# Three of the five shared-expert down products made inside the expert loop, kept in SBUF, and added by VectorE at the end

## The chip, the cores and the metric

One core of a Trainium2 chip runs the whole program. The time is the device time of one execution in microseconds (us); lower is better. TensorE is called PE here, VectorE DVE, ScalarE ACT, GpSimd POOL, and SyncE, whose queue issues most of the large DMAs, SP.

## What is computed

One layer of a decoder trunk over 512 prompt tokens and 8 sample tokens, 1024 wide: a token mixer with two gated convolution branches, then a mixture of experts with 64 routed experts (8 for each token) and one shared expert. All in float32. The part that the change touches is the end of the second half:

```
hg = jnp.einsum('td,edf->tef', h, p['w1'])
hu = jnp.einsum('td,edf->tef', h, p['w3'])
act = jax.nn.silu(hg) * hu * gate[:, :, None].astype(h.dtype)
routed = jnp.einsum('tef,efd->td', act, p['w2'])
shared = (jax.nn.silu(h @ p['ws1']) * (h @ p['ws3'])) @ p['ws2']
return routed + shared
...
x = x + gt2 * rmsnorm(f, p['g_post2'])
```

## The kernel before

The program has a first half (projections, convolutions, router), an expert loop and a tail. Each engine has its own program; they meet at semaphores.

**The expert loop.** The rows of each expert are cut into strips of 64, and one pass handles two strips that follow each other (128 rows). For these inputs there are 49 passes. In a pass, POOL gathers the rows from `h2_rows` into `xg`; PE transposes them (`rows_T`, L1684) into PSUM banks 0 and 1; PE makes the up products with w1 and w3 (`up_product`, L1691) into banks 2 and 3, transposes the gated result (`act_T`, L1697) into banks 6 and 7, and makes the down products with w2 (`down_products`, L1703) into banks 4 and 5. ACT evicts those, and POOL scatters them to `y_rows` in HBM. PE's code for this loop is `for u in range(DEEP): expert(g * DEEP + u, u, g)` in a hardware loop over `g` of 10 turns: six bodies written out one behind the other, one for each slot of weights, and four more bodies for the last four experts. A body is skipped where its expert has no pass to make, and repeated where it has several. Which experts have how many passes follows from the routing of the inputs.

**The weights.** SP loads 3 MB for each expert (`up_weights`, two DMAs of 1 MB at L351; `down_weights`, one at L356) into six slots. `refill` waits until the expert six back has finished (semaphores `ex3` and `ex_y` against a pass number) before it overwrites that slot.

**The shared expert.** Its up products and gating are done before the loop; the result waits in `scr`. Its down products (`shared_down`, L1770, 4 matrix products of 128 x 128 by 128 x 512 for each token tile) are made in the tail, where PE opens the PSUM sum of each tile with them. `ws2` (1 MB) is loaded at L410, late in the loop, into a slot that is free by then.

**The tail.** There are five token tiles: four of 128 prompt tokens and one of 8 sample tokens. Tile n has two PSUM banks, `bank_of = (6, 0, 2, 4, 6)`. PE adds to the shared product the gated rows that were scattered to `y_rows`: eight rows a token, in a first and a last half (`gated_rows`, L1778, with h=1 from `y_first` and h=0 from `y_last`), each half a load of 2 MB by `tile_rows` (L406) into places in the weight slots. For each finished tile ACT squares and sums (L987) and takes the root (L990), DVE takes the reciprocal (L1363), scales (L1369) and adds the residual (L1372), and SP stores it (L452). SP's loads wait for the last pass that wrote rows of the tile (`rows_there`), for the slot (`slot_free`), and where a place is used twice, for PE's `early_pe`.

Of the kernel before, what the change touches and what calls it, by code (L numbers as in the profile page):

```python
# [10 lines left out]
ALU = mybir.AluOpType  # L11
ACT = mybir.ActivationFunctionType
AX = mybir.AxisListType
ds = bass.ds
# [8 lines left out]
def build_program(  # L23
# [33 lines left out]
    with ctx:  # L57
# [64 lines left out]
        hx = ring[:, 0, 4 * D:6 * D].rearrange("p (b d) -> p b d", b=2)  # L122
        hflat = act5[:, R:2 * R]
        yb = hflat[:, 2 * D:4 * D].rearrange("p (b d) -> p b d", b=2)
        gmat = hflat[:, 0:D].rearrange("p (b i h m) -> p b i h m", b=4, i=TT - 1, h=2)
        xflat = act5[:, 0:R]
# [12 lines left out]
        sel, selm, repl = (xflat[:, o + n * RE:o + (n + 1) * RE].rearrange("p (i e) -> p i e", i=TT) for n in range(3))  # L139
# [21 lines left out]
        outb = [hflat[:, D:2 * D], slot_part(4, YF, D), slot_part(4, YF + D, D)]  # L161
# [60 lines left out]
        def s8(n):  # L222
# [45 lines left out]
                 "m_hi_dve x1_pool gp_pe gm_dve early_dve early_pe last_pass_dve x1t_T x1t_done x1t_dve h2_dve oneE_dve token_act turn_pool sh_mm sh_ev sh_act "  # L268
# [34 lines left out]
        def _(sp):  # L303
# [71 lines left out]

            def refill(e, before, u):
# [33 lines left out]
            sp.dma_start(ws2_back, w_src(ws2, 0, D)).then_inc(w_late, 16)  # L410
            slot_free(E - 5)
            x1_back(0)
            x1_back(1)
# [10 lines left out]
            for i in range(3):  # L424
                tile_rows(y_first, i, 1, y_first_in)
# [3 lines left out]
            tile_rows(y_first, 3, 1, y_first_in)  # L429
# [3 lines left out]
            sp.dma_start(G2, g2_rows[0:1, :].to_broadcast([P, D])).then_inc(g2_in, 16)  # L433
            rows_there(1)
            tile_rows(y_last, 0, 0, y_last_in[0])
            slot_free(E - 2)
            sp.dma_start(G2s, g2_rows[1:NSEQ, :]).then_inc(g2_in, 16)
            rows_there(2)
            tile_rows(y_last, 1, 0, y_last_in[1])
            rows_there(3)  # L440
            slot_free(E - 1)
            tile_rows(y_last, 2, 0, y_last_in[2])
            rows_there(4)
            sp.wait_ge(S["early_pe"], 1)
            tile_rows(y_last, 3, 0, y_last_in[3])
# [216 lines left out]
        def _(act):  # L662
# [321 lines left out]
            for n in range(TT):  # L984
                rows, f = (P if order[n] < TT - 1 else LAST), bank_of[n]
                act.wait_ge(S["stat_mm"], 3 * C + n + 3)
                act.activation(sflat[0:rows, 0:D], ps[0:rows, f:f + 2, :].rearrange("p b n -> p (b n)"), ACT.Square,  # L987
# [5 lines left out]
        def _(dve):  # L993
# [287 lines left out]
            link(dve.tensor_reduce(red[0:1 + TT, 2:3], ps[0:1 + TT, 6, 0:P], AX.X, ALU.max), "early_dve", wait=False)  # L1281
            tile_no = dve.alloc_register("tile_no")
            dve.reg_mov(tile_no, 0)

# [37 lines left out]
            link(ts(last_pass, ps[0:1, 6, P:P + 1 + TT], 4.0 * P - 1.0, None, ALU.add), "early_dve")  # L1322
# [14 lines left out]
            with dve.Fori(0, pairs) as it:  # L1337
                for u in range(2):
# [18 lines left out]

            for n in range(TT):
                i, f = order[n], bank_of[n]
                rows = P if i < TT - 1 else LAST  # L1360
                buf, r = outb[n % 3][0:rows, :], nrm[0:rows, 1, n:n + 1]
# [7 lines left out]
                stt(out=buf, in0=ps[0:rows, f:f + 2, :].rearrange("p b n -> p (b n)"), scalar=r, in1=(G2 if i < TT - 1 else G2s)[0:rows, :],  # L1369
# [5 lines left out]
        def _(pe):  # L1375
# [344 lines left out]
            for n in range(3):  # L1720
                pe.reg_load(next_steps[n], steps_of[0:1, n:n + 1])
# [121 lines left out]
```

## Time and profile before

| | us |
|---|---|
| median of 3 runs | 1288.71 |
| lowest and highest | 1286.37 and 1288.80 |
| the profiled execution, device time | 1286.83 |
| its span in the profile | 1285.1 |
| expert loop, first to last matrix product of PE | 644.1 to 1242.4 |
| tail, to the end | 1242.4 to 1285.1 |

"Idle before" in a row is time in which that engine had nothing to run just before those instructions, with what ended it. "Issue" is time in which the engine waited for nothing that the profile shows. PEld is PE's weight load, which overlaps PE; PEldq and PEq are its sequencer. A busy PE in the profile counts pipelined matrix products, so it can read 100% of a stretch. The DMA share is the mean busy share of 16 DMA engines. An instruction packet (queue q8) brings 16 KB of PE's code, 256 instructions of 64 bytes. The program's instructions by the written order are 7517 for PE, 29.4 packets, and 29 packets are seen.

### The profile page before, as it was taken

How to read it: one execution, taken by the hardware profiler on the slowest of the kernel's cores; microseconds unless marked ns; L12 is line 12 of the kernel's file. 1: busy time of each engine (PE TensorE's matmuls, PEld its weight loads, DVE VectorE, ACT ScalarE, POOL GpSimd, SP SyncE). 2: the span in 40 equal slices, each digit the busy share in tenths (PEclk: the TensorE clock that was granted, in tenths of full speed). 3: DMA queues.
4: the chain of work that ended last, by engine and by line, in shares of the span. 5: the costliest groups of instructions: out<-in, count | busy, mean ns of one | idle time of the engine just before them, and what ended most of it. 6: DMA issues, size and time to landing. Idle time of an engine off the chain costs nothing.

```text
span 1285.1 us, 26379 instructions
## 1 busy us (share of the span) xinstructions
PE 1222.1 (95%) x9371; PEld 912.3 (71%) x9372; DVE 466.3 (36%) x840; ACT 344.5 (27%) x628; POOL 375.6 (29%) x380
## 2 busy tenths in 40 slices
PE   5699999999999999977999999999799999999997
PEld 4599999999999999966755655555455565555552
DVE  0566686658566538226722111101000100110114
ACT  4332322322333531335211212112112121211212
POOL 1144544445447234320412122122112212212210
PEclk9799999999999999987989999999899999999999
DMA  9944253452421133408699999999999999999883
GB/s 305 291 159 153 83 194 103 147 159 82 147 82 49 34 104 93 132 1 322 260 360 382 369 365 420 391 418 418 418 417 418 391 406 361 416 419 410 340 339 141
DMA packets 157770, 337.33 MB, mean 262 GB/s; under 512 B 12390, under 2 KB 96870, under 8 KB 141328
## 3 DMA queue, kind: packets, MB, share of 16 engines
q1 hardware_dynamic: 140048, 295.55, 61.2%
q0 software_dynamic: 14256, 34.10, 7.0%
q10 hardware_dynamic: 3424, 7.09, 1.7%
q8 instruction: 29, 0.48, 0.2%
q14 instruction: 13, 0.11, 0.0%
HBM read 322.21 MB, written 33.30 MB: 277 GB/s over the span
## 4 chain that ended last, share of the span: by engine, by line
PE 82%; DMA 5%; issue 5%; DVE 4%; POOL 2%; SPq 1%; ACT 1%; DVEq 0%; ACTq 0%; POOLq 0%
PE ps L1691 26%; PE ps L1703 13%; PE ps L1456 10%; PE ps L1457 9%; PE ps L1458 9%; PE ps L1684 4%; DMA w<-in_w_dram 2%; DMA ring<-in_w_ada_dram 2%; PE ps L1770 1%; PE ps L1469 1%; PE ps L1697 1%; PE ps L1411 1%; PE ps L1778 1%; PE ps L1636 1%; PE ps L1399 1%
## 5 line engine op out<-in xcount | busy, mean ns | idle before, releaser
L1691 PE MATMUL ps<-w,xe 128*64 x3136 | 351.4, 383 | 12.8 <-DMA w<-in_w_dram 8.9
L1691 PEld LDWEIGHTS ps<-w,xe 128*64 128x64 f32 x3136 | 228.1, 138 | 148.5 <-issue 44.7
L520 POOL TENSOR_TENSOR wsplit<-ring,wsplit 128x1024 fp32r<-128x1024 f32 x80 | 192.2, 2402 | 302.4 <-ACT wsplit L713 302.4
L1456 PE MATMUL ps<-h_s_hi,wsplit 128*128 128x260 f32 x960 | 272.2, 284 | 0.0
L1458 PE MATMUL ps<-h_s_hi,wsplit 128*128 128x260 f32 x960 | 270.7, 282 | 0.0
L1457 PE MATMUL ps<-h_lo_m_hi,wsplit 128*128 128x260 f32 x832 | 234.8, 282 | 0.0
L1334 DVE TENSOR_TENSOR rs<-sg,ps 128x128 f32<-128x128 f32 x98 | 23.8, 284 | 480.8 <-PE ps L1691 480.8
L1456 PEld LDWEIGHTS ps<-h_s_hi,wsplit 128*128 128x128 f32 x960 | 180.6, 188 | 6.7 <-issue 6.7
L1458 PEld LDWEIGHTS ps<-h_s_hi,wsplit 128*128 128x128 f32 x960 | 180.8, 188 | 0.0
L1703 PE MATMUL ps<-w,eactT 128*64 (+1 forms) x784 | 179.0, 598 | 0.0
L713 ACT ACTIVATE wsplit<-ring 128x1024 fp32r<-128x1024 f32 x80 | 84.8, 1060 | 310.1 <-PE ps L1458 294.2
L1457 PEld LDWEIGHTS ps<-h_lo_m_hi,wsplit 128*128 128x128 f32 x832 | 156.6, 188 | 0.0
L1072 DVE SCALAR_TENSOR_TENSOR ps<-conv,vecs,ps 128x512 f32<-128x512 f32 x224 | 154.7, 745 | 0.0
L595 POOL COPY gidx<-idxT 128x1 int32 (+1 forms) x50 | 9.4, 189 | 395.7 <-PE ps L1684 394.3
L1703 PEld LDWEIGHTS ps<-w,eactT 128*64 128x64 f32 x784 | 52.2, 136 | 89.7 <-issue 83.7
L955 ACT ACTIVATE act<-ps 128x1024 f32<-128x1024 f32 x50 | 51.2, 1023 | 162.9 <-PE ps L1703 147.3
L970 ACT ACTIVATE eactT<-ps 128x128 f32<-128x128 f32 x98 | 23.3, 277 | 188.6 <-PE ps L1697 188.6
L1684 PE MATMUL ps<-ident,scr 128*128 128x128 f32 x400 | 65.7, 287 | 0.0
L1684 PEld LDWEIGHTS ps<-ident,scr 128*128 128x128 f32 x400 | 52.3, 193 | 18.9 <-issue 17.7
L598 POOL DMA_INDIRECT scr<-h_rows,gidx x50 | 53.1, 1063 | 39.7 <-POOL gidx L595 39.7
L608 POOL DMA_INDIRECT y_rows<-act,sidx x49 | 50.4, 1028 | 40.3 <-POOL sidx L605 32.1
L967 ACT ACTIVATE sg<-ps 128x256 f32<-128x256 f32 x49 | 18.8, 384 | 134.5 <-PE ps L1691 132.0
(315 smaller groups left out, 1363.3 us busy)
## 6 DMA issues: line engine op xcount, KB each, us to landing
w<-in_w_dram SPq DMA_DIRECT2D x192, 1024.0 KB, 15.3
ring<-in_w_in_dram SPq DMA_DIRECT2D x56, 512.0 KB, 3.7
ring<-in_w_ada_dram SPq DMA_DIRECT2D x12, 2048.0 KB, 8.9
act<-y_rows SPq DMA_DIRECT2D x4, 2048.0 KB, 10.2
ring<-y_rows SPq DMA_DIRECT2D x4, 2048.0 KB, 9.5
ring<-in_w_out_a_dram SPq DMA_DIRECT2D x8, 512.0 KB, 3.5
ring<-in_w_out_b_dram SPq DMA_DIRECT2D x8, 512.0 KB, 3.6
ring<-in_w_o_dram SPq DMA_DIRECT2D x8, 512.0 KB, 3.5
```

What stands on the lines that cost most here:

```text
L520: pool.tensor_tensor(wsplit[:, b, 1], raw[raw_slot], wsplit[:, b, 0], ALU.subtract).then_inc(S["w_lo"], 1)
L598: pool.indirect_dma_start(out=xg, out_offset=None, in_=h2_rows, in_offset=bass.IndirectOffsetOnAxis(ap=gidx[:, u:u + 1], axis=0), bounds_c ...
L608: pool.indirect_dma_start(out=y_rows, out_offset=bass.IndirectOffsetOnAxis(ap=sidx[:, u:u + 1], axis=0), in_=yb[:, u, :], in_offset=None, ...
L713: act.activation(wsplit[:, b, 0], raw[raw_slot], ACT.Copy).then_inc(S["w_hi"], 1)
L955: act.activation(yb[:, 1 - u, :], ps[:, 4:6, :].rearrange("p b n -> p (b n)"), ACT.Copy).then_inc(S["ex_yd"], 1)
L1072: chain(stt(out=acc[k % 2] if k != KC - 2 else cvj, in0=glu[:, k:k + NP], scalar=vecs[:, ds(j + (V_WC + 8 * k), 1)], in1=acc[k % 2], op0=A ...
L1456: mm(ps[:, bank + h, 0:HT], wsplit[:, b, 0, k, :], hi[:, k, p:q], start=(k == 0), stop=False)
L1457: mm(ps[:, bank + h, 0:HT], wsplit[:, b, 0, k, :], lo[:, k, p:q], start=False, stop=False)
L1458: ins = mm(ps[:, bank + h, 0:HT], wsplit[:, b, 1, k, :], hi[:, k, p:q], start=False, stop=(k == C - 1))
L1684: ins = tr(ps[:, h, (c % 4) * P:(c % 4 + 1) * P], v[:, c, :], ident[:, :])
L1691: ins = mm(ps[a * STRIP:(a + 1) * STRIP, bank, 0:FE], xe[:, k, a * STRIP:(a + 1) * STRIP], w[a][:, k, :], start=(k == 0), stop=(k == C - 1))
L1703: ins = mm(ps[a * STRIP:(a + 1) * STRIP, 4 + h, :], eactT[:, k, a * STRIP:(a + 1) * STRIP], w[a][:, k, h * 512:(h + 1) * 512], start=(k == ...
```

## The change

`ws2` is loaded before the loop, into two new places, instead of late in it. In passes 11, 12 and 13 (p = 10, 11, 12) PE makes the down products of token tiles 1, 2 and 3 behind the down products of the pass, into PSUM banks 6 and 7, and DVE copies them to SBUF (`xflat`). Each of the ten bodies of PE's code holds the three products behind comparisons with the pass number. In the tail `gated_rows` opens the PSUM sum of tiles 1 to 3, and DVE adds the parked product to it; the sum stands in SBUF, and ACT and DVE read it from there. Tiles 0 and 4 are made as before. The places of `y_first` and `y_last` move: the second half of tile 1 is now in slot 4, and the second halves of tiles 2 and 3 in slots 5 and 0, each behind one step of `early_pe`. Names of semaphores change with that (`early_dve` is now `sums_dve`).

```diff
-        y_first = [blocks(t) for t in (xflat[:, 0:YF], slot_part(5, 0, YF), slot_part(0, 0, YF), slot_part(1, 0, YF))]
-        y_last = [blocks(t) for t in (slot_part(2, 0, YF), slot_part(3, 0, YF), slot_part(4, 0, YF), xflat[:, 0:YF])]
-        ws2_back = slot_part(5, YF, 2 * D).rearrange("p (k n) -> p k n", k=FT)
+        y_first = [blocks(slot_part(n, 0, YF)) for n in (5, 0, 1, 2)]
+        y_last = [blocks(slot_part(n, 0, YF)) for n in (3, 4, 5, 0)]
+        FIRST_SH = 10
+        SH_TILES = TT - 2
...
             sp.wait_ge(S["table_dve"], 1)
 
+            for k in range(FT):
+                sp.dma_start(ws2_late[k], ws2[0, k * P:(k + 1) * P, :]).then_inc(w_late, 16)
+
...
-            sp.dma_start(ws2_back, w_src(ws2, 0, D)).then_inc(w_late, 16)
...
-            rows_there(4)
-            sp.wait_ge(S["early_pe"], 1)
-            tile_rows(y_last, 3, 0, y_last_in[3])
+            for i in range(2, TT - 1):
+                rows_there(i + 1)
+                sp.wait_ge(S["early_pe"], i - 1)
+                tile_rows(y_last, i, 0, y_last_in[i])
...
                     one_pass(p)
+                    with dve.If(it > FIRST_SH // 2 - 1):
+                        with dve.If(it < FIRST_SH // 2 + 2 - u):
+                            n = dve.snap(shared_no, min_val=1, max_val=SH_TILES)
+                            dve.wait_ge(S["late_chain"], LA * TT)
+                            dve.wait_ge(S["sh_mm"], n + 2 * FT)
+                            dve.tensor_copy(xflat[:, ds(n * D - D, D)], ps[:, 6:8, :].rearrange("p b n -> p (b n)")).then_inc(S["sums_dve"], 1)
+                            dve.wait_ge(S["sums_dve"], n + 2)
+                            dve.reg_add(shared_no, shared_no, 1)
...
+            def with_shared(n):
+
+                if n > SH_TILES:
+                    return
+                f, total = bank_of[n], xflat[:, (n - 1) * D:n * D]
+                dve.wait_ge(S["stat_mm"], 3 * C + n + 3)
+                tt(total, total, ps[:, f:f + 2, :].rearrange("p b n -> p (b n)"), ALU.add).then_inc(S["sums_dve"], 1)
+
             for n in range(TT):
                 i, f = order[n], bank_of[n]
                 rows = P if i < TT - 1 else LAST
+                if n > 0:
+                    with_shared(n + 1)
...
+            def shared_in_loop(i):
+
+                pe.wait_ge(w_late, 16 * C + 64)
+                for h in range(2):
+                    for k in range(FT):
+                        ins = mm(ps[:, 6 + h, :], scr[:, 2 + k, i * P:(i + 1) * P], ws2_late[k][:, h * 512:(h + 1) * 512],
+                                 start=(k == 0), stop=(k == FT - 1))
+                ins.then_inc(S["sh_mm"], 1)
...
                         down_products(down, 1).then_inc(S["ex_y"], 1)
+                        with pe.If(p > FIRST_SH - 1):
+                            with pe.If(p < FIRST_SH + SH_TILES):
+                                with pe.If(p < FIRST_SH + 1):
+                                    shared_in_loop(1)
+                                with pe.If(p > FIRST_SH):
+                                    with pe.If(p < FIRST_SH + 2):
+                                        shared_in_loop(2)
+                                    with pe.If(p > FIRST_SH + 1):
+                                        shared_in_loop(3)
...
             pe.wait_ge(S["xe_dve"], passes + 1)
-            shared_down(1)
+            mark(gated_rows(1, 1, y_first), "early_pe")
             last_sums(0)
-            gated_rows(1, 1, y_first)
             pe.wait_ge(S["ex_yd"], passes + 2)
             for n in range(2, TT - 1):
-                shared_down(n)
+                gated_rows(n, 1, y_first)
                 last_sums(n - 1)
-                gated_rows(n, 1, y_first)
```

On PE, at the end of each body of the expert loop, before (L1703 are the down products, L1730 and L1729 the ends of the pass loop and of the body):

```order
L1703 ISA [waits ea_act]
L1703 MATMUL ps<-w,eactT 64x512 x2
L1703 ISA
L1703 MATMUL ps<-w,eactT 64x512 x2
L1730 REGISTER_ALU
L1730 COMPARE_AND_BRANCH
L1729 UNCONDITIONAL_BRANCH
```

The same place now (L1736 are the down products, L1761 the shared ones):

```order
L1736 MATMUL ps<-w,eactT 64x512 x2
L1797 COMPARE_AND_BRANCH
L1798 COMPARE_AND_BRANCH
L1799 COMPARE_AND_BRANCH
L1761 MATMUL ps<-act,scr 128x512 [waits w_late]
L1761 MATMUL ps<-act,scr 128x512 x3
L1799 UNCONDITIONAL_BRANCH
L1801 COMPARE_AND_BRANCH
L1802 COMPARE_AND_BRANCH
L1761 MATMUL ps<-act,scr 128x512 [waits w_late]
L1761 MATMUL ps<-act,scr 128x512 x3
L1802 UNCONDITIONAL_BRANCH
```

Behind these rows stands a third copy (L1804), and then the loop ends as before. A product of this kind is four instructions on the engine (two weight loads and two matrix products), so a body grows by 48 of them and 9 branches, from 221 to 278 instructions.

On PE in the tail, before, from the shared product of tile 0 on:

```order
L1770 MATMUL ps<-act,scr 128x512 [waits w_late]
L1770 MATMUL ps<-act,scr 128x512 x3
L1778 MATMUL ps<-act 32x512 [waits y_first_in,gm_dve]
L1778 MATMUL ps<-act 32x512 x7
L1800 REGISTER_ALU
L1770 MATMUL ps<-act,scr 128x512 [waits xe_dve,xe_act]
L1770 MATMUL ps<-act,scr 128x512 x3
L1778 MATMUL ps<-ring,act 32x512 [waits y_last_in0]
L1778 MATMUL ps<-ring,act 32x512 x7
L1778 MATMUL ps<-act 32x512 x8
L1805 REGISTER_ALU
L1770 MATMUL ps<-act,scr 128x512 [waits ex_yd]
```

And now:

```order
L1821 MATMUL ps<-act,scr 128x512 [waits w_late]
L1821 MATMUL ps<-act,scr 128x512 x3
L1829 MATMUL ps<-act 32x512 [waits y_first_in,gm_dve]
L1829 MATMUL ps<-act 32x512 x7
L1851 REGISTER_ALU
L1829 MATMUL ps<-ring,act 32x512 [waits xe_dve,xe_act]
L1829 MATMUL ps<-ring,act 32x512 x7
L1829 MATMUL ps<-ring,act 32x512 [waits y_last_in0]
L1829 MATMUL ps<-ring,act 32x512 x7
L1855 REGISTER_ALU
L1829 MATMUL ps<-ring,act 32x512 [waits ex_yd]
```

The shared products of tiles 1 to 3 are gone from between the gated rows; that of tile 4 stays.

## Rows read from the trace of the kernel before

**Rows 1.** The page: span, busy time of PE, and PE's code packets.

```profile
span 1285.1 us, 26379 instructions
PE 1222.1 (95%) x9371; PEld 912.3 (71%) x9372; DVE 466.3 (36%) x840; ACT 344.5 (27%) x628; POOL 375.6 (29%) x380
...
q8 instruction: 29, 0.48, 0.2%
```

**Rows 2.** Chain that ended last, passes 47 and 48: start us, us, what.

```profile
1218.55 6.91 PE ps L1691 x64
...
1230.48 6.91 PE ps L1691 x64
```

**Rows 3.** Chain that ended last, tail.

```profile
1243.59 3.63 PE ps L1770 x8
...
1252.71 3.57 PE ps L1778 x32
...
1275.90 1.12 ACT scr L987 x2
```

**Rows 4.** Groups by line, 1242 to 1286: busy us, mean ns, idle before.

```profile
L1369 DVE SCALAR_TENSOR_TENSOR act<-ps,nrm,ring 128x1024 f32<-128x1024 f32 (+1 forms) x5 | 6.4, 1281 | 0.2
L1372 DVE TENSOR_TENSOR act<-act,ring 128x1024 f32<-128x1024 f32 (+1 forms) x5 | 6.1, 1223 | 0.2
```

**Rows 5.** Chain around the wait for weights.

```profile
873.36 6.91 PE ps L1691 x64
...
888.86 28.71 DMA w<-in_w_dram
918.27 9.11 PE ps L1691 x64
...
932.41 6.91 PE ps L1691 x64
```

**Rows 6.** Loads of weights issued at 713 and at 827: median us to landing.

```profile
w<-in_w_dram SPq DMA_DIRECT2D x2, 1024.0 KB, 8.7
...
w<-in_w_dram SPq DMA_DIRECT2D x3, 1024.0 KB, 12.3
```

**Rows 7.** Stretches: busy us of each engine, PE's clock, DMA share, GB/s.

```profile
749.00:755.00 6.00, 6.00 (x38) 3.16 (x38) 1.74 (x7) 1.77 (x4) 2.44 (x4) 1.00 0.80 319
791.00:803.00 12.00, 12.00 (x94) 6.95 (x92) 1.18 (x3) 2.37 (x5) 2.44 (x4) 1.00 1.02 419
```

**Rows 8.** Loads in 1242 to 1275: median us from issue to landing.

```profile
act<-y_rows SPq DMA_DIRECT2D x2, 2048.0 KB, 10.2
```

**Rows 9.** PE's code packets: 0 to 136, 640 to 700, 646.5 to 648.

```profile
q8 instruction: 7, 0.11, 0.4%
...
q8 instruction: 5, 0.08, 0.6%
...
q8 instruction: 1, 0.02, 4.9%
```

**Rows 10.** Queues of 136 to 411 us, then of 700 to 1188: all there are.

```profile
q1 hardware_dynamic: 48878, 32.51, 37.9%
...
q1 hardware_dynamic: 30173, 169.37, 85.3%
q0 software_dynamic: 11554, 27.20, 14.4%
```

**Rows 11.** Branches that skip a body, at 643 and at 1192: ns min/median/max, start us.

```profile
L1729 PEldq COMPARE_BRANCH  x2: 70/204/337, 643.0 to 643.6; - x2
L1729 PEldq COMPARE_BRANCH  x2: 65/196/328, 1192.0 to 1192.5; - x2
```

**Rows 12.** DMA of 1193 to 1195 us: PE's code packet.

```profile
q8 instruction: 1, 0.02, 3.3%
```

**Rows 13.** Line 1691 in pass 48: matrix products, and the sequencer's work for them.

```profile
L1691 PE MATMUL ps<-w,xe x64: 379/379/379, 1230.3 to 1237.0; 128*64 x32, 128*64 128x256 f32 x32
L1691 PEldq FUSED_REGOPS  x16: 42/46/51, 1228.0 to 1234.6; - x16
```

More of the change, by code:

```diff
@@ L138, in build_program @@
         o += 4 * TT * 8
-        sel, selm, repl = (xflat[:, o + n * RE:o + (n + 1) * RE].rearrange("p (i e) -> p i e", i=TT) for n in range(3))
+        repl, sel, selm = (xflat[:, o + n * RE:o + (n + 1) * RE].rearrange("p (i e) -> p i e", i=TT) for n in range(3))
         rank1, place_of = sel, repl
@@ L267, in build_program @@
                  "g_done m_done m_chain t_cp stat_mm sqd idx_ab idx_mm hx_T hx_done "
-                 "m_hi_dve x1_pool gp_pe gm_dve early_dve early_pe last_pass_dve x1t_T x1t_done x1t_dve h2_dve oneE_dve token_act turn_pool sh_mm sh_ev sh_act "
+                 "m_hi_dve x1_pool gp_pe gm_dve sums_dve early_pe last_pass_dve x1t_T x1t_done x1t_dve h2_dve oneE_dve token_act turn_pool sh_mm sh_ev sh_act "
                  "exT xe_act xe_dve ex1 ex3 ex_sil ex_mul exA ea_act "
@@ L423, in _ @@
             rows_there(0)
-            for i in range(3):
-                tile_rows(y_first, i, 1, y_first_in)
+            tile_rows(y_first, 0, 1, y_first_in)
+            slot_free(E - 5)
+            x1_back(0)
+            x1_back(1)
+            tile_rows(y_first, 1, 1, y_first_in)
             slot_free(E - 4)
@@ L985, in _ @@
                 rows, f = (P if order[n] < TT - 1 else LAST), bank_of[n]
-                act.wait_ge(S["stat_mm"], 3 * C + n + 3)
-                act.activation(sflat[0:rows, 0:D], ps[0:rows, f:f + 2, :].rearrange("p b n -> p (b n)"), ACT.Square,
+                if 1 <= n <= SH_TILES:
+                    act.wait_ge(S["sums_dve"], 2 + SH_TILES + n)
+                    total = xflat[:, (n - 1) * D:n * D]
+                else:
+                    act.wait_ge(S["stat_mm"], 3 * C + n + 3)
+                    total = ps[0:rows, f:f + 2, :].rearrange("p b n -> p (b n)")
+                act.activation(sflat[0:rows, 0:D], total, ACT.Square,
                                accum_out=nrm[0:rows, 0, n:n + 1]).then_inc(S["fin_sq"], 1)
@@ L1280, in _ @@
             link(tt(first_at, beyond, one64[0:1, :], ALU.add), "table_dve")
-            link(dve.tensor_reduce(red[0:1 + TT, 2:3], ps[0:1 + TT, 6, 0:P], AX.X, ALU.max), "early_dve", wait=False)
+            link(dve.tensor_reduce(red[0:1 + TT, 2:3], ps[0:1 + TT, 6, 0:P], AX.X, ALU.max), "sums_dve", wait=False)
             tile_no = dve.alloc_register("tile_no")
             dve.reg_mov(tile_no, 0)
+            shared_no = dve.alloc_register("shared_no")
+            dve.reg_mov(shared_no, 1)
             def token_tile(i, u):
@@ L1368, in _ @@
                     dve.wait_ge(tile_out[n % 3], 16)
-                stt(out=buf, in0=ps[0:rows, f:f + 2, :].rearrange("p b n -> p (b n)"), scalar=r, in1=(G2 if i < TT - 1 else G2s)[0:rows, :],
+                total = xflat[:, (n - 1) * D:n * D] if 1 <= n <= SH_TILES else ps[0:rows, f:f + 2, :].rearrange("p b n -> p (b n)")
+                stt(out=buf, in0=total, scalar=r, in1=(G2 if i < TT - 1 else G2s)[0:rows, :],
                     op0=ALU.mult, op1=ALU.mult).then_inc(S["yacc"], 1)
@@ L1372, in _ @@
                 tt(buf, buf, x1b[i][0:rows, :], ALU.add).then_inc(S["fin_out"], 1)
+                if n == 0:
+                    with_shared(1)
         @block.tensor
@@ L1769, in shared_down @@
                     for k in range(FT):
-                        mm(ps[0:rows, f + h, :], scr[:, 2 + k, i * P:i * P + rows], ws2_back[:, k, h * 512:(h + 1) * 512],
+                        mm(ps[0:rows, f + h, :], scr[:, 2 + k, i * P:i * P + rows], ws2_late[k][:, h * 512:(h + 1) * 512],
                            start=(k == 0), stop=False)
@@ L1778, in gated_rows @@
                         ins = mm(ps[32 * b:32 * b + 32, f + c, :], gmat[:, b, i, h, :], src[i][:, b, c * 512:(c + 1) * 512],
-                                 start=False, stop=(h == 0))
+                                 start=(h == 1 and 1 <= n <= SH_TILES), stop=(h == 0))
                 return ins
@@ L1794, in _ @@
             mark(ins, "gp_pe")
-            pe.wait_ge(w_late, 16 * C + 48)
+            pe.wait_ge(w_late, 16 * C + 64)
             shared_down(0)
```

26 lines of the change are left out of this document (12 added, 14 removed).

## Prediction

> **What bounds the kernel now.** I read the page first. PE is busy 95% of the span, DVE 36% and POOL 29% [rows 1], so the question is what PE gains, loses or waits for. Then the chain that ended last. In the expert loop it runs through PE's products, one pass starting 11.93 us after the one before (1230.48 − 1218.55) [rows 2]; 49 passes at 11.92 make 584 us of the 598.3 us from 644.1 to 1242.4. Of the other 14 us some 11.4 stand at one place: four passes from 873.36 to 932.41 take 59.05 us and not 47.7, because PE waits for a load of weights that took 28.71 us, and the products behind it take 9.11 us instead of 6.91 at a lower clock [rows 5]. In the tail the chain is PE again, shared and gated products one behind the other, until ACT squares the last tile at 1275.90, 33.5 us after the loop's end [rows 3]. Behind it ACT and DVE need 9.2 us to the end.
>
> So work taken out of the tail's PE chain shows there. Work put into passes 11 to 13 shows in full, unless the wait for weights at 890 swallows it.
>
> **The work put into the loop.** A shared product is 8 matrix products, 3.63 us in the tail [rows 3]. Three are 10.9 us. PE has no gap in those passes: the chain of the later passes has none [rows 2], and in 791 to 803 PE is busy 12.00 of 12.00 us [rows 7]. So passes 11 to 13 grow from 11.9 to 15.5 us.
>
> Does the wait for weights absorb that? The bounds are 10.9 (nothing) and −0.5 (it hands over all of its 11.4). In favour of absorbing: 85 us later PE waits for a transfer anyway. Against: SP issues a load only when PE has finished the expert six back, so PE's delay delays the issues, and the DMA engines absorb it only as far as transfers are queued. That backlog is read from the time from issue to landing: 8.7 us for loads issued at 713, 12.3 at 827 [rows 6]. So some 3.6 us are queued by then; the rest of the 10.9 us the DMA engines stand idle, and what they don't move in time is missing at 890. I take 10.9 − 3.6 = **+7.3 us**.
>
> Three smaller edits I cost at nothing, with their cover. The comparisons: one to nine branches for each pass, 65 to 70 ns where not taken and 328 to 337 ns where taken [rows 11]; PE's sequencer ends its work for L1691 at 1234.6, when the products end at 1237.0 [rows 13], a lead of 2.2 to 2.4 us, and uncovered they would be about 0.3 us a pass (49 × 0.3 = 15 us, which I don't expect). DVE's copy of 128 x 1024 from PSUM is like L1372 (1.22 us [rows 4]); DVE is idle most of a pass, and banks 6 and 7 are wanted again by PE's `act_T` over 7 us later; the wait for `sh_mm` has only the next pass's gating queued behind it, and that needs products which PE makes later. The early load of `ws2`: 1 MB, some 2.5 us of all engines at 419 GB/s; the DMA share is 0.80 in 749 to 755 [rows 7], so room is there before anything waits, and its late load is gone.
>
> **The tail.** PE loses three products, 3 × 3.63 = 10.9 us: the last sum is ready 22.6 us after the loop's end instead of 33.5. DVE gets three additions of 128 x 1024 (1.22 to 1.28 us each [rows 4]), the one for tile n+1 in front of the scaling of tile n. With PE sending a tile every 3.57 us [rows 3] and DVE needing 0.17 + 1.28 + 1.22 + 1.25 = 3.9 us for each, DVE becomes the engine that sets the pace from tile 1 to 3. Laid out by hand: the additions and the slower pace cost 2.8 us of the 10.9, so the tail gains **8.1 us**. The loads of gated rows are next in line. One took 10.2 us [rows 8]; the second half of tile 1 now waits for the last pass and lands about 8 us behind the loop's end (wanted at 12), that of tile 2 at 14 (wanted at 15.7), tile 3 at about 20 (wanted at 21). They just hold. Bounds: 10.9 if the additions vanish in gaps, 5 if the loads come 3 us late.
>
> **The sum without anything else** is +7.3 − 8.1 = −0.8 us: nothing.
>
> **PE's code.** The change also makes the loop's code longer, and that I take to decide. The code comes in packets of 256 instructions [rows 9]. Counted in the written order, the first half's loop lies from 1.6 to 7.3 packets behind the start: 7 packets, and one more that is called ahead. 7 came in 0 to 136 us [rows 9] and one at its exit; in 136 to 411 none came [rows 10]. The six bodies of the expert loop lie from 19.3 to 24.5: 6 packets and one called ahead. Five came in 640 to 700 [rows 9], and none in 700 to 1188, while ten turns run [rows 10]. So eight packets are the most that a row shows held. With 278 instructions for a body instead of 221 the loop lies from 19.3 to 25.8. The real borders lie earlier than the count: packets start to come when PE is at about 160 of 256, with its lead at about 196, so at least 60 instructions (0.24 packets) separate the count from the real border, and the loop ends at 26.06 or later. That touches 8 packets and calls a ninth.
>
> If a ninth pushes out the oldest, that is the packet with the loop's start, and each of the 9 jumps back waits for it. When it has come, it pushes out the next, and so on, but those are called ahead while 1.3 passes of work are left. So the waits are at the jumps: 9 back, and those over the sixth body where that expert has no pass (6 of 10 turns by the routing), since they land in a packet not yet called. The price from the trace: the jump at 643.0 [rows 11], with no packet until 646.5 and then one that took 4.9% of 16 engines times 1.5 us = 1.18 us [rows 9], 4.7 us in all; the jump at 1192.0 [rows 11], with none until 1193 and one of 3.3% of 16 × 2 = 1.07 us [rows 12], 2.4 us in all. Mean 3.5 us. At a jump back the sequencer's lead of 2.2 us [rows 13] covers a part: 9 × 1.3 = 12 us. At a jump over a body the lead has been used on other branches, and I take all 3.5: 6 × 3.5 = 21 us. Together **+33 us**. Bounds: 0 if nothing is pushed out, 10 if only jumps back pay, and 60 where each fetch stands behind the loads of a saturated DMA (share 1.02 in 791 to 803 [rows 7]).
>
> The Trainium skill, "Runtime: NRT & Kernel Launch", Instruction fetch mechanics, says that PE's instruction memory has 128 KiB, 2048 instructions, filled first in, first out in blocks of 16 KiB, and that a taken branch to a page not held forces a fetch before execution goes on. That is eight packets, and the loop without refetches of nine would contradict it. The same section also says that only two lines are held; by that every turn of before would refetch too, and [rows 10] show no packet in ten turns, so here the trace decides against it.
>
> **Rivals.** *Nothing is refetched* (more than eight are held, or the real end of the loop stays in the packet before): the sum is −0.8 us, 1286 to 1288. For it: the overshoot is small, 0.06 packets by my count, and no row shows a refusal of nine. *Nothing refetched, and the wait for weights swallows the added work*: −0.5 − 8.1 = −8.6, so 1278 to 1280, faster. For it is the 11.4 us stretch [rows 5]; against it the small backlog [rows 6]. *Every packet of each turn comes late*, because fetches stand behind a full DMA: 10 turns × 6 to 8 us, over 1345. The code decides over the sign: the forecast ends on the slower side from the point where jumps cost more than 0.2 us each.
>
> **How the numbers follow.** The profiled execution took 1286.83 us, 1.9 below the median of the runs; I sum against it. Forecast: 1286.83 + 7.3 − 8.1 + 33 = **1319 us**. Chances: refetches at jumps 0.50 (about 1295 to 1335 with its bounds), nothing refetched 0.28, nothing refetched and the wait swallows 0.12, all late 0.10. The range of 1284 to 1345 leaves out the last case and most of the third. A measurement of this kernel can tell 0.2% (2.6 us) from no change; by that: faster 0.15 (the third case and a little of the second), same 0.20, slower 0.65. If only the signs hold, the forecast's own range is 1295 to 1335.
>
> **What would show it.** Code packets of PE on the page: about 31 if nothing is refetched, 60 to 100 if it is, and some between 700 and 1188. The first pass of a turn starting more than 11.93 us after the one before, by 1 to 4 us, and PE idle there with nothing that the profile shows ("issue"). Passes 11 to 13 at 15.5 us. The wait for weights, 11.4 us long now, shorter by about 3.6. The tail from the loop's end to the end 34.6 us instead of 42.7, DVE's additions at about 1.25 us, and PE not waiting for gated rows. I am wrong if the packets stay at 31: then the time is that of the rivals, and their order is settled by the start of the last pass.

## The result, and the profile after

The changed kernel takes 1292.62 us (median of 7 runs, 1291.28 to 1293.2), the kernel before 1288.31 us (7 runs): a ratio of 1.0036, 95% interval 1.0026 to 1.0046, 4.3 us slower. The profiled executions took 1292.62 and 1286.83 us; the latter is one of the faster ones of its kernel, so the two traces lie 5.8 us apart. The sign is the forecast one, the size is about a seventh of the 32 us that were forecast, and the cause is another one.

The page of the changed kernel, as [rows 1]:

```profile
span 1290.9 us, 26586 instructions
PE 1224.0 (95%) x9371; PEld 913.0 (71%) x9372; DVE 473.2 (37%) x846; ACT 344.4 (27%) x628; POOL 376.3 (29%) x380
...
q8 instruction: 31, 0.51, 0.2%
```

31 code packets for 31.4 in the written order: no packet came twice. The queues of 700 to 1188 us, as [rows 10]; there is no q8 among them:

```profile
q1 hardware_dynamic: 29562, 166.21, 84.2%
q0 software_dynamic: 11317, 26.63, 14.2%
```

So the 33 us that the prediction put on refetched code are not there. Where the 5.8 us are is read from the starts of the passes (first product of L1691, now L1724, in each pass of both traces):

| | before | after | moved by |
|---|---|---|---|
| first pass starts | 644.14 | 644.44 | +0.30 |
| pass 11 starts (two steps, at passes 5 and 9) | 765.90 | 766.63 | +0.73 |
| pass 14 starts (11.3 us lost in three passes) | 801.67 | 813.71 | +12.04 |
| pass 21 starts | 885.11 | 897.22 | +12.11 |
| pass 25 starts (behind the wait for weights) | 944.16 | 954.34 | +10.18 |
| pass 45 starts | 1182.62 | 1192.84 | +10.22 |
| pass 46 starts | 1194.54 | 1207.28 | +12.74 |
| loop ends | 1242.4 | 1255.2 | +12.8 |
| tail, from there to the end | 42.7 | 35.7 | −7.0 |

Four lines of it are the case: the products cost 11.3 us, the wait for weights gives 1.9 back, 2.5 are lost at the loop's exit, and the tail gains 7.0. The 0.7 us of the first passes are no part of it: in the profiles of the kernels below, those with added copies of code aside, pass 11 starts 0.3 to 3.7 us behind before, in no relation to the edits.

The chain in passes 11 and 12 of the changed kernel (start us, us, what), beside [rows 2]:

```profile
775.13 3.58 PE ps L1736 x16
778.72 3.63 PE ps L1761 x8
782.35 7.06 PE ps L1724 x64
...
794.42 3.63 PE ps L1761 x8
```

A product is 3.63 us, as forecast, and the up products behind it take 7.06 us instead of 6.91: 3.77 a pass. DVE's copy (3 of 1225 ns) and the branches are hidden.

The wait for weights, as [rows 5]:

```profile
901.99 25.45 DMA w<-in_w_dram
927.43 0.66 issue
928.10 9.47 PE ps L1724 x64
```

It is still there, and the low clock behind it too (9.47 us for the up products; the granted clock is 0.72 in 922 to 934). PE waited 6.5 us for weights in the loop, against 8.9 before.

At the loop's exit PE's sequencer shows the loss. The branches that skip a body in the code behind the loop (now L1771), at 1202.6 and 1206.7 us, as [rows 11]:

```profile
L1771 PEldq COMPARE_BRANCH  x2: 82/1964/3846, 1202.6 to 1206.7; - x2
```

One branch took 3.85 us where the same one took 0.33 before. A code packet arrives meanwhile (one starts at 1203.8 in the trace and takes 1.27 us); PE's next product starts at 1207.28 after 2.35 us of "issue".

The tail's chain ends otherwise than before:

```profile
1257.39 7.33 DMA y_rows<-act,sidx
...
1265.30 12.04 DMA ring<-y_rows
...
1277.38 1.97 PE ps L1829 x16
...
1279.38 1.22 DVE act L1384
...
1287.31 1.21 DVE act L1403
```

In [rows 3] it ran through PE's products; now it is the last scatter, then the last load of gated rows, then DVE's addition. PE waits 1.83 us for that load.

### The profile page after: what moved, and what is told of

Its sections match the earlier page's. It is cut to its first block, busy times and chain, and to the rows that moved or that the text cites. A ratio compares the mean times of both kernels' runs of the same rounds, so it can differ in the third digit from the quotient of the medians.

```text
span 1290.9 us, 26586 instructions
## 1 busy us (share of the span) xinstructions
PE 1224.0 (95%) x9371; PEld 913.0 (71%) x9372; DVE 473.2 (37%) x846; ACT 344.4 (27%) x628; POOL 376.3 (29%) x380
## 4 chain that ended last, share of the span: by engine, by line
PE 79%; DMA 8%; issue 5%; DVE 4%; POOL 2%; SPq 1%; ACT 1%; DVEq 0%; POOLq 0%; ACTq 0%
PE ps L1724 25%; PE ps L1736 13%; PE ps L1489 9%; PE ps L1490 9%; PE ps L1491 9%; PE ps L1717 4%; DMA w<-in_w_dram 2%; DMA ring<-in_w_ada_dram 2%; DMA scr<-h_rows,gidx 1%; PE ps L1502 1%; PE ps L1730 1%; PE ps L1444 1%; PE ps L1669 1%; PE ps L1432 1%; SPq L313 1%
## 5 line engine op out<-in xcount | busy, mean ns | idle before, releaser
L1724 PE MATMUL ps<-w,xe 128*64 x3136 | 352.0, 383 | 12.9 <-DMA w<-in_w_dram 6.5
L1724 PEld LDWEIGHTS ps<-w,xe 128*64 128x64 f32 x3136 | 227.9, 138 | 149.5 <-issue 46.1
L1736 PE MATMUL ps<-w,eactT 128*64 (+1 forms) x784 | 179.0, 598 | 0.0
L1736 PEld LDWEIGHTS ps<-w,eactT 128*64 128x64 f32 x784 | 52.2, 136 | 89.9 <-issue 84.1
```

The lines of the kernel that those rows point to most:

```text
L1724: ins = mm(ps[a * STRIP:(a + 1) * STRIP, bank, 0:FE], xe[:, k, a * STRIP:(a + 1) * STRIP], w[a][:, k, :], start=(k == 0), stop=(k == C - 1))
L1736: ins = mm(ps[a * STRIP:(a + 1) * STRIP, 4 + h, :], eactT[:, k, a * STRIP:(a + 1) * STRIP], w[a][:, k, h * 512:(h + 1) * 512], start=(k == ...
```

## Experiments

Each ratio is against runs of the kernel before made beside that kernel's own. "Changed kernel" is the kernel of the diff.

### Do the products alone make the loss?

The passes at which PE's products are made are set out of reach, so the kernel leaves the shared part of tiles 1 to 3 out of its output:

```diff
-                        with pe.If(p > FIRST_SH - 1):
+                        with pe.If(p > NEVER - 1):
...
-  dve.wait_ge(S["sh_mm"], n + 2 * FT)
-  dve.tensor_copy(xflat[:, ds(n * D - D, D)], ps[:, 6:8, :]...)
+  dve.wait_ge(w_late, 16 * C + 64)
+  dve.tensor_copy(xflat[:, ds(n * D - D, D)], ws2_late[0])
```

> The code of the three products stays in all bodies, but the comparisons never hold: no shared product of tiles 1 to 3 is made, so this part of the output is left out; DVE parks other data with a copy as long as before, and the tail is the changed one. Theory (the time of the changed kernel is products in the loop, less a little swallowed by the wait for weights, plus one late code packet at the loop's exit, less the tail): the loop's passes 11 to 13 are back at 11.92 us, the last pass starts about 11.3 - 1.9 = 9.4 us earlier than in the changed kernel, near 1233.7; the 2.4 us gap before pass 46 is still there, since the code is as long; time about 1292.6 - 9.4 = 1283. Rival (branches and early ws2 cost much of it): last pass at 1236 or later, time 1285 or more.

Measured: 1279.45 us, ratio 0.9933 (0.9916 to 0.9949). No pass reaches the number 100, and it is past the bound that the program states for the pass number: the comparisons and the products' code were dropped when the kernel was built, so the code is short again, which the page shows:

```profile
q8 instruction: 29, 0.48, 0.2%
```

The last pass starts at 1232.0, 11.1 us earlier than in the changed kernel; that is 1.7 us behind before, and it was 1.9 us behind at its first pass already. The gap before pass 46, which the expectation kept, is gone with the code. So early `ws2` and the moved loads cost nothing that can be seen in the loop. DVE's copies were not as long as before, against the expectation: from SBUF they take 683 ns each, and from PSUM in the changed kernel 1225. The whole kernel is 1288.11 − 1279.45 = 8.7 us faster than before by the medians; in the two profiles its tail is 7.4 us shorter (35.3 against 42.7). The products and their code cost 13.2 us against it. The run mixes these two causes; the next runs part them.

### The gap at the loop's exit

```diff
-            def expert(e, u, turn):
+            def expert(e, u, turn, with_products=True):
...
+                        if with_products:
                             with pe.If(p > FIRST_SH - 1):
...
-                expert(E // DEEP * DEEP + u, u, E // DEEP)
+                expert(E // DEEP * DEEP + u, u, E // DEEP, False)
```

> The changed kernel without the products' code in the four bodies behind the loop, where no pass 11 to 13 falls. Theory (PE waits at the loop's exit because a skipped body is now longer than a packet of 256 instructions, 278, and lands in a packet that was not called): the skip takes 0.33 us again instead of 3.85, pass 46 starts 11.9 us after pass 45 instead of 14.4, the time falls by 2.4 us to about 1290.2. Rival (the gap comes from where the loop's end lies against the packets, or from a full DMA queue, not from the length of the skipped body): the gap stays between 1 and 3 us.

Measured: 1290.08 us, ratio 1.0018 (1.0009 to 1.0028), 2.5 us below the changed kernel. Pass 46 starts 11.92 us after pass 45, and the same branches read:

```profile
L1771 PEldq COMPARE_BRANCH  x2: 65/196/328, 1202.1 to 1202.7; - x2
```

The six bodies of the loop are unchanged and the loop ends at the same place of the code, so the longer bodies behind the loop make the gap: the skip over one of them finds its packet not there yet, and with the short bodies it doesn't. That a length above 256 instructions alone decides is not shown. In the first turn of the changed kernel the skip over the sixth body, as long as the others, did not wait:

```profile
L1771 PEldq COMPARE_BRANCH  x1: 338/338/338, 692.6 to 692.6; - x1
```

The edit changes the length of the body and the place at which the skip lands together, and no run parts the two.

### Where the products stand before the wait for weights

`FIRST_SH` alone is changed: 10 in the changed kernel; 14, 18 and 20 here. "Still to come" is what the products do to the passes behind the start of pass 21.

```diff
-        FIRST_SH = 10
+        FIRST_SH = 18
```

> The products are made in passes 19 to 21 (p = 18 to 20), just ahead of the wait for weights. Theory (a delay of PE is swallowed only when loads are queued behind each other, since each load is issued when PE has finished a pass; at p = 10 little was queued, at p = 18 the loads take over 17 us from issue to landing): the wait swallows most of the 11.3 us, up to the 9.3 us that it lasts and 2.2 us of low clock; the last pass starts about 8 us earlier than in the changed kernel, the time is 1283 to 1286. Rival (the DMA engines bound this stretch whatever PE does, and later loads come later by as much, or PE's delay comes back as a second wait): the same loop as the changed kernel within 2 us, time 1291 to 1293.

> The products are made in passes 21 to 23 (p = 20 to 22): the first two fill the very gaps in which PE waits for weights (3.3 us and 6.0 us), the third comes behind them. Theory as in the run before it: no refill that feeds the two waits is delayed, so 3.3 + 3.8 us are swallowed at once, and of the third product and of what stays of the second gap some 4 us are paid; the last pass starts 5 to 8 us earlier than in the changed kernel, time 1284 to 1288. Rival (a later wait takes the place of the removed one): time 1291 to 1293, with a wait for weights after pass 24.

> The products are made in passes 15 to 17 (p = 14 to 16). Theory (what the wait for weights swallows is what is queued when the products are made; loads take 11.9 us from issue to landing at 820 and 16 to 17 at 860, against 8 when nothing is queued): between the two cases measured, 3 to 6 us swallowed, last pass near 1239 to 1241, time 1287 to 1290. Rival (swallowed is all or nothing, by whether the products stand inside some 40 us ahead of the wait): as passes 11 to 13, time 1291 to 1293.

| products in passes | behind before at pass 21, and still to come | behind before at pass 25 | swallowed | median us | ratio (95%) |
|---|---|---|---|---|---|
| 11 to 13 | 12.1 | 10.2 | 1.9 | 1292.6 | 1.0036 (1.0026 to 1.0046) |
| 15 to 17 | 11.7 | 2.1 | 9.6 | 1284.4 | 0.9973 (0.9961 to 0.9985) |
| 19 to 21 | 9.3 + 3.8 | 1.8 | 11.3 | 1284.2 | 0.9973 (0.9961 to 0.9984) |
| 21 to 23 | 1.1 + 11.3 | 2.3 | 10.1 | 1286.1 | 0.9977 (0.9965 to 0.9990) |

With the products in passes 19 to 21 the wait is gone from the chain (to be read beside [rows 5]): a product stands where PE waited, the next up products start on time, and the 6.91 us of the pass behind them are those of the full clock. (This profile is of the slowest of ten runs, 1288.05 us. Behind the stretch shown it has a tail of 37.8 us, where the other profiles of changed kernels have 33 to 36.)

```profile
906.55 3.63 PE ps L1761 x8
910.18 7.06 PE ps L1724 x64
...
918.67 3.58 PE ps L1736 x16
922.26 6.91 PE ps L1724 x64
```

The rival, a wait that comes back later, fell for passes 19 to 21: from pass 22 on all passes take 11.92 to 11.97 us up to the loop's exit. The expectation for passes 15 to 17 was too careful: 9.6 us were swallowed, not 3 to 6. What differs is read from the DMA share (last two columns: share, GB/s). The kernel before, 814 to 826:

```profile
814.00:826.00 12.00, 12.00 (x94) 6.96 (x92) 1.18 (x3) 2.45 (x6) 2.53 (x5) 1.00 0.95 377
```

The changed kernel, from 802 on:

```profile
802.00:814.00 12.00, 12.00 (x68) 5.79 (x66) 1.24 (x4) 2.06 (x5) 2.44 (x4) 1.00 0.88 327
814.00:826.00 12.00, 12.00 (x94) 6.99 (x92) 2.34 (x4) 1.45 (x5) 1.95 (x4) 1.00 0.57 214
826.00:838.00 12.00, 12.00 (x94) 6.96 (x92) 1.18 (x3) 2.45 (x6) 2.53 (x5) 1.00 0.88 323
838.00:850.00 12.00, 12.00 (x94) 6.94 (x92) 1.18 (x3) 2.45 (x6) 2.50 (x5) 1.00 1.00 390
```

Products in passes 15 to 17:

```profile
838.00:850.00 12.00, 12.00 (x69) 5.71 (x70) 1.92 (x2) 1.88 (x3) 2.44 (x4) 1.00 0.99 405
850.00:862.00 12.00, 12.00 (x67) 5.79 (x64) 1.99 (x4) 1.99 (x4) 2.44 (x4) 1.00 0.76 259
```

Products in passes 19 to 21, while they are made:

```profile
900.00:912.00 12.00, 12.00 (x68) 5.77 (x64) 2.40 (x4) 1.99 (x4) 2.44 (x4) 1.00 1.02 417
```

A full share reads 1.02 here. The changed kernel falls short of it by 0.14, 0.45, 0.14 and 0.02 in four windows of 12 us, 9 us in all (before loses 1.1 there as well); passes 15 to 17 lose about 3.5 in the two windows shown and 0.7 behind them; passes 19 to 21 lose nothing. What was swallowed goes the other way (1.9, 9.6, 11.3), and the two add up to some 10 to 14 us each time: PE's delay of 11.3 us either leaves DMA engines idle or is swallowed. And the kernel before dips to 0.95 at 814 to 826, before any delay: the engines are a little short of work there already, and in the changed kernel no load of weights at all is in flight from 818.6 to 826.0. Products ahead of that dip (11 to 13) pass most of their delay on to the weights (9.4 of 11.3 us); products behind it, where loads queue up again, don't.

### Both edits together, and two tiles in place of three

> The two edits that helped are put together: products in passes 19 to 21, and no product code in the four bodies behind the loop. Theory (they remove separate losses: the 11.3 us that the wait for weights now swallows, and the code packet at the loop's exit with the low clock behind it, 2.4 + 1.7 us in the run of passes 19 to 21): pass 46 starts 11.92 us after pass 45, the last pass starts near 1232, the time is 1279.5 to 1281, 0.994 of the kernel before. Rival (the freed time is lost again in the tail, because the last load of gated rows ends the chain there): the same last pass, but a tail of 38 us, time 1283.

Measured: 1280.39 us, ratio 0.9936 (0.9922 to 0.9949): 0.6% below the kernel before and 12 us below the changed one. Pass 46 starts on time, the last pass starts at 1231.6, and the tail is 35.5 us. The two losses were separate ones. This kernel is called the fast version below.

The next kernel makes two of the products in the loop:

```diff
-        SH_TILES = TT - 2
+        SH_TILES = TT - 3
...
-                                    with pe.If(p > FIRST_SH + 1):
-                                        shared_in_loop(3)
...
             for n in range(2, TT - 1):
+                if n > SH_TILES:
+                    shared_down(n)
                 gated_rows(n, 1, y_first)
```

> As the run before it, but only tiles 1 and 2 have their products made in the loop; that of tile 3 is made in the tail as before, where PE otherwise waits some 2 us for the last load of gated rows. Theory (the tail ends with that load, and behind it DVE's addition for tile 3 stands on the chain): PE's wait is filled, its clock does not fall, the addition of 1.22 us is gone, the loop is the same since the wait for weights swallows two or three products alike; the tail is 34 to 35 us, the time 0 to 1.5 us below that of the run before it. Rival (PE is the later one in the tail again): the tail 1.5 to 2 us longer than there.

Measured: 1279.88 us, ratio 0.9935 (0.9920 to 0.9950), the same as with three tiles. The tail is 35.1 us instead of 35.5, its chain runs through PE again without a wait for a load, and the addition is gone from it. In the loop PE comes to the wait for weights with one product less, and waits there. From its chain:

```profile
920.61 25.15 DMA w<-in_w_dram
945.76 0.70 issue
946.46 8.81 PE ps L1724 x64
```

The last pass of this profile starts 2.9 us later than with three products (1234.4 against 1231.6), but 2.6 us of that stand there at pass 12, before any product. Counted from pass 19 both versions swallow theirs: two products leave 0.3 us at pass 26, three leave nothing. So three products fit the wait, the loop gains nothing from making one less, and the expectation was right for the loop and nearly so for the tail (34 to 35 us).

### What the additions cost in the tail

ACT and DVE read PSUM in the next kernel, and `with_shared` does nothing, so it leaves the shared part of tiles 1 to 3 out of its output. Then the addition for tile 3 is moved behind the scaling of tile 2, in the fast version:

```diff
-                if n > 0:
+                if 0 < n < SH_TILES - 1:
                     with_shared(n + 1)
...
-                if n == 0:
-                    with_shared(1)
+                if n == 0 or n == SH_TILES - 1:
+                    with_shared(n + 1)
```

> The changed kernel, but DVE does not add the parked products, ACT and DVE read PSUM: the shared part of tiles 1 to 3 is left out of the output. Theory (the tail's end is set by the last load of gated rows, so DVE's slower pace in the middle costs nothing and only the last addition stands on the chain): the tail is 1.2 to 1.5 us shorter than in the changed kernel, 34.3 us, time 1291.2. Rival, the prediction's term (DVE sets the pace from tile 1 on, the additions cost 2.8 us): the tail 2.8 us shorter, time 1289.8.

> The version with products in passes 19 to 21 and short bodies behind the loop; in DVE's code of the tail the addition for tile 3 now stands behind the scaling of tile 2, not ahead of it. Theory (DVE works in order, so while PE waits for the last load of gated rows the scaling of tile 2, 2.7 us, is held up behind an addition that can't start, and then runs in series behind it): what follows the landing of that load is 1 to 1.3 us shorter, 12.3 us instead of 13.6; time 1279.2, against 1280.4. Rival (tile 2's work only fills time in which DVE would wait for ACT's sum of squares of tile 3): no change beyond 0.3 us.

Without additions: 1289.92 us, ratio 1.0017 (1.0008 to 1.0026), 2.7 us below the changed kernel, tail 33.1 us instead of 35.7. That is the size that the prediction gave them (2.8 us, named as the rival here; 1.2 to 1.5 were expected), but not for its reason. The chain still ends with the load, and what follows it is shorter:

```profile
1264.92 11.76 DMA ring<-y_rows
1276.68 0.04 issue
1276.72 1.97 PE ps L1825 x16
```

From its landing at 1276.68 to the end (1287.92) it is 11.2 us; in the changed kernel, from 1277.34 to 1290.89, it is 13.5. DVE's pace in the middle of the tail costs nothing, since it waits there (3.29 us before the last addition); the 2.3 us are the addition (1.22) and the scaling of tile 2 that stands behind it in DVE's order, though its data were ready. DVE in the fast version, first with the old order and then with the new:

```profile
1267.67 1.22 DVE L1384 TENSOR_TENSOR act<-act,ps 128x1024 f32<-128x1024 f32 x1 [2.10 <-PE ps L1830]
1268.81 0.15 DVE L1393 RECIPROCAL nrm<-nrm 128x1 f32<-128x1 f32 x1
```

```profile
1269.85 1.22 DVE L1384 TENSOR_TENSOR act<-act,ps 128x1024 f32<-128x1024 f32 x1
1272.61 0.16 DVE L1393 RECIPROCAL nrm<-nrm 128x1 f32<-128x1 f32 x1 [1.54 <-ACT nrm L1000]
```

With the new order the addition starts without a wait, but DVE then waits 1.54 us for ACT's root. From landing to end it is 12.9 us instead of 13.5, 0.7 less before rounding where 1 to 1.3 were expected, and the median is 1280.67 (ratio 0.9944, 0.9931 to 0.9958) against 1280.39: no difference that these runs can tell.

### Was the code near a limit?

No refetch was seen, but that does not say whether the mechanism exists. So the six bodies were made longer by copies that never run, in the fast version:

```diff
+                            with pe.If(p > STEPS - 2):
+                                for _ in range(1):
+                                    shared_in_loop(1)
                             with pe.If(p > FIRST_SH - 1):
```

> The same version with two more copies of the product's code in each of the six bodies, behind a comparison that never holds: the loop's code lies from 19.3 to 26.6 packets in the written order, so it touches eight packets and its end calls a ninth. The prediction's step (a ninth packet pushes out the loop's first, and each of nine jumps back waits for it): packets between 700 and 1188, passes longer by 1 to 4 us at the starts of turns, time 1290 to 1313. Rival (the ninth is not called, or pushes out one that is not needed): 31 or 32 packets on the page, none between 700 and 1188, time 1280.4 within 1 us.

> As the run before it with five more copies: the loop lies from 19.3 to 27.7, nine packets touched and a tenth called. The prediction's step: packets are fetched in every turn, 60 or more on the page, the passes at the jumps back longer by 1 to 4 us; time 1290 to 1320. Rival (more than eight are held): no packet between 700 and 1188 and 1280.4 within 1 us.

> The version with products in passes 19 to 21 and short bodies behind the loop, with one more copy of the product's code in each of the six bodies, never run: the loop lies from 19.3 to 26.2 packets, between the changed kernel's 25.8, which fetches nothing, and 26.6, which fetches in every turn. Theory A (a loop may touch no more than seven packets by the written order, as the first half's loop from 1.6 to 7.3 and the changed kernel's do; the eighth, number 26, is one too many): fetches in every turn, some 60 packets between 700 and 1188, time about 1425. Theory B (eight may be touched, and it is the call for a ninth, which only a loop's end near 26.6 makes, that pushes out the first): none between 700 and 1188, 30 or 31 on the page, time 1280 to 1281.

| loop's code, in packets from the start | packets touched | on the page | between 700 and 1188 | median us |
|---|---|---|---|---|
| 19.29 to 25.82 (three copies) | 7 | 30 | 0 | 1280.4 |
| 19.29 to 26.24 (one more) | 8 | 104 | 59 | 1413.0 |
| 19.29 to 26.61 (two more) | 8 | 105 | 63 | 1425.4 |
| 19.29 to 27.74 (five more) | 9 | 122 | 68 | 1461.0 |

The places are counts in the written order of each program. The ratios are 1.0965 (1.0946 to 1.0984), 1.1063 (1.1046 to 1.1080) and 1.1355 (1.1326 to 1.1383). The page of the kernel with one more copy:

```profile
q8 instruction: 104, 1.70, 0.5%
```

Its first jump back, at 698.1, and the chain at the second jump back of the kernel with two more:

```profile
L1811 PEldq COMPARE_BRANCH  x1: 7302/7302/7302, 698.1 to 698.1; - x1
```

```profile
772.46 3.58 PE ps L1736 x16
776.05 11.19 issue
787.23 8.51 PE ps L1724 x64
```

In these three kernels 26 of the 27 jumps back wait 5.7 to 7.9 us for their packet, skips over a body up to 7.3 us, and the up products behind such a wait take 8.5 to 10.1 us from first to last, instead of 7.1. What the 133 us of the kernel with one more copy are made of shows in its loop (second row), beside that of the version without copies (first row; us of PE's products, last columns clock, DMA share, GB/s):

```profile
644.00:1247.00 603.00, 600.92 (x4451) 346.12 (x4452) 76.66 (x190) 118.60 (x248) 120.70 (x195) 1.00 0.98 391
644.00:1379.00 735.00, 629.95 (x4450) 358.67 (x4451) 75.47 (x187) 117.46 (x247) 119.36 (x194) 0.93 0.84 321
```

The products take 29 us longer, at a granted clock of 0.93 instead of 1.00, and PE stands idle about 103 us more: its waits of "issue" ahead of up products are 106.2 us (19 of them), against 4.0 (one).

Theory A of the last expectation fits: the kernels whose loop touches seven packets fetch nothing in it, those that touch eight do, and the forecasts for the first two kernels (up to 1313 and 1320 us) were far too low. Three things stay open. One jump back of nine in the kernel with one more copy took 0.21 us (at 965.8), so eight packets don't miss every time. The length grows with the count of packets (6.5 packets without fetches, 6.95 with them), and no loop was moved against the borders at one length, so that touching an eighth packet decides, and not the length, is not shown. And the counts are somewhat high: the written order has unconditional branches in each body, of which no trace shows PE execute one. The built code has 273 instructions in a body of the changed kernel and 219 before, not 278 and 221, and the loops of the table end at 25.69, 26.09, 26.46 and 27.59; the packets touched are the same. The changed kernel ends its loop 46 instructions ahead of the next border by the written order (0.18 × 256), 79 by the built code.

The Trainium skill, "Runtime: NRT & Kernel Launch", Instruction fetch mechanics, gives 128 KiB for PE, refilled in 16 KiB blocks, and a forced fetch for a branch to what is not held. The forced fetch agrees with these rows. Its two-page window does not: loops that touch seven packets fetched nothing in ten turns. Nor is it enough here to stay below the 2048 instructions that 128 KiB are: the loop with one more copy has fewer than 1800 (6.95 × 256) and fetched.

## Why the prediction was wrong

- **Product in the loop, 3.63 us each, all of it on PE:** right for the product; 11.3 us instead of 10.9, because the up products behind it take 0.15 us more.
- **The wait for weights absorbs 3.6 us:** the mechanism was right (a load is issued when PE has finished, so PE's delay empties the queue) and the size was not: 1.9 us. The failing step was to read the backlog as the difference of two latencies in [rows 6], 12.3 − 8.7. The DMA share of before shows it more directly: 0.95 at 814 to 826, engines short of work before any delay. The term was to be +9.4 us and not +7.3.
- **Branches, copies and early `ws2` at nothing:** nothing in the runs speaks against it: outside the waits and the first two turns, passes without a product take 11.92 to 11.98 us in the changed kernel, against 11.92 to 11.94 before, and the 0.4 us that its first two turns add are less than the profiles differ there.
- **Tail −8.1 us:** measured −7.0 between the two profiles, −7.4 in the profile of the first experiment (whose medians differ by 8.7 as a whole). The price of the additions (2.8) was met by 2.7, the place was not: "DVE sets the pace" was wrong, the loads "just hold" was wrong by 1.8 us. The last load took 12.0 us from issue to landing and not 10.2. Why is not shown: the load of tile 2 still ran beside it, but it did so too in the version with two tiles, where the same load took 10.5.
- **PE's code, +33 us: the step that failed.** The prediction took the loop to reach into an eighth packet and to call a ninth, and put 33 us on it; the trace has no fetch in the loop, 0 us. It had moved all borders 0.24 packets earlier and so had the loop's end at 26.06. The counts as they stand (25.82, seven packets) fit all six loops. Whether the shift itself was wrong is open: by the built code's 273 instructions a body the loop ends at 25.69, and with the shift at 25.93, still in the seventh. The 0.06 packets of overshoot were smaller than the error of the count. The second part, "a ninth pushes out the oldest", is not what the runs show either: with eight touched the first jump back already waits, and between the packet at 695.6 and the one at 701.3, which comes for the jump at 698.1, no other came. The mechanism itself is real, and its price was set too low by a factor of four: 133 us where 33 were forecast. The two jumps from which 4.7 and 2.4 us were read had not waited: they took 0.34 and 0.33 us, and the passes behind them started at 644.14 and on time at 1194.54, so these were times of fetches and not prices of jumps. The median jump back takes 7.2 us and not 3.5, skips over other bodies than the sixth wait too, and the clock falls. A slip in the recorded bounds changes nothing: 60 us on −0.8 give 1346 us, not 1335.
- **Not foreseen:** a skip over one of the longer bodies behind the loop, 2.5 us once, at the loop's exit.

The rival "nothing is refetched" gave 1286 to 1288, and that is what came true of the code; its time was still 4 us too low or more. With its two wrong terms put right (+9.4 instead of +7.3, −7.0 instead of −8.1, and +2.5 at the exit) and the 0.7 us of the first passes, the sum is 1286.83 + 11.3 − 1.9 + 2.5 + 0.7 − 7.0 = 1292.4, against 1292.62 in the profiled execution. The terms are read from the same two traces, so the sum shows that nothing large is left out and is no test of them. That the measured time lies inside 1284 to 1345 is the width of that range and not the forecast: the 33 us were not there.

## What to carry to other kernels

Work moved from a tail into a loop is free only where the loop already waits, and where the DMA engines between that place and the wait never run short of work: look at the DMA share just behind the place, not at the latency of single loads. Count the packets of 256 instructions that a hardware loop touches, in the code as built, before adding to its body: here one copy of 16 instructions and its branch, six times over, took the time from 1280.4 to 1413.0 us, and it never ran. Code that a place can't need is best left out of it: taking it from four bodies gave 2.5 us.

## What the runs showed of the hardware

- Loops on PE that touch up to seven code packets (6.5 packets long at most) fetched nothing in their turns. One that touches eight (6.95 long) fetched 59 packets in 488 us, and branches that found their packet missing took up to 7.9 us. The rule between (which packet goes, when the next is called, and whether places or length decide) is not settled by these runs.
- PE's clock fell behind short waits, in the rows by their times: 8.81 us for up products that take 7.08 (their span in the timeline) at the loop's exit of the run with passes 19 to 21, after a wait of 2.21 us, with a granted clock of 0.86 in the window of 1196 to 1208. The timeline's row, and the window's:

```profile
1198.88 8.81 PE L1724 MATMUL ps<-w,xe 128*64 x64 [2.21 <-issue]
```

```profile
1196.00:1208.00 12.00, 9.79 (x71) 5.90 (x68) 0.19 (x1) 1.41 (x2) 1.01 (x1) 0.86 0.93 358
```

- The changed kernel has the same wait (2.35 us) and no fall behind it: up products of 7.13 us, a granted clock of 1.00 in its window of 1196 to 1208. What decides between the two is open.
